# Shifting where the tensor engine's operands begin inside a 256-byte period of SBUF

## The chip, the cores and the metric

The kernel runs on one core of one Trainium2 chip. The metric is the device time of one execution in microseconds (us): the median over the runs shown, beside one profiled execution from which all rows below come.

## The reference, cut to what matters

Two transformer blocks in sequence, on one sequence of 512 tokens with model width 1024, in float32. The first block has four attention branches (stick-breaking, block-sparse, forgetting, top-k), gates on them, and a feed-forward net with a convolution of three taps. The second block is run for two layers: a feed-forward net, a mixer with four parts (latent attention, spatial gating, a gated recurrence, retention), a second feed-forward net and a gated side input.

```python
y = sigmoid(xn @ w_gate[i]) * (merge_heads(branches[i]) @ w_branch[i])     # first block, i = 0 to 3
hdn = xn @ w_up                                                            # 1024 -> 5632, then conv, gelu, @ w_down
h = h + 0.5 * swiglu(rmsnorm_2(h, ffn1_norm[l]), w_gate[l], w_up[l], w_down[l])   # twice a layer, 1024 -> 2816 -> 1024
z = rmsnorm_2(h, mix_norm[l]) @ w_in[l]
```

By far most of the arithmetic is the product of the 512 tokens with weight matrices.

## The kernel before, in words

**The weight stream.** All weights of the networks and projections are cut into 504 pieces of 128 partitions x 1024 floats (4096 bytes of a partition). SyncE (SP) loads a piece into one of two slots of `raw`, by two DMAs (`piece`, L494), as soon as the piece two before it has been split. GpSimd (POOL) splits it: L678 rounds `raw` into `wh` (type fp32r), L685 writes the rest `raw - wh` into `wl`, in four instructions of 256 columns. Both have two slots. TensorE (PE) then multiplies. The activations are split in the same way into a rounded part and a rest: `xh` and `xl` for the normed input, `op_hi` and `op_lo` for four more rows of operands, and areas of the large buffer `arena` (under its second name `arena_rounded`) for `yh`, `yl`, `mh`, `ml` and most of the hidden rows of the networks. Each product of a block of 128 weights' columns with 512 tokens is three matmuls of fp32r: `wh` with the rounded part, `wh` with the rest, `wl` with the rounded part. These are L728, L729 and L737 (`products`), L1269, L1270 and L1277 (the down projections), L775, L776 and L780 (`fm_steps`), L850, L851 and L858, L1180, L1181 and L1187. In L876, L877 and L885 the roles are exchanged: the stationary operand is a block of tokens and the moving one a block of 2 x 128 weights.

Every such matmul has a weight load of its own (LDWEIGHTS, 128 x 128), which runs while the matmul before it streams.

**Other work on TensorE.** Attention, the recurrence, transposes and sums of squares take their operands from `arena`, `const` and `ones` as plain float32.

**What sets the order.** The order on each engine is written out by hand; engines wait for each other by semaphores. The lists `BEHIND`, `AHEAD` and `LAST` say which piece's product stands behind which step of the attentions. Piece by piece, POOL's L678 waits for the DMAs of its piece and for PE's last use of `wh` two pieces ago (`rounded_read`), L685 for PE's last use of `wl` two pieces ago (`pieces_used`), PE for POOL.

**Where things lie.** The tensors are allocated one behind another in SBUF, each beginning at a multiple of 32 bytes. What follows calls the remainder of a beginning by 256 bytes its *residue*. Rows of 512 floats and blocks of 128 or 1024 floats are multiples of 256 bytes, so inside `wh`, `wl`, `xh`, `xl`, `op_hi`, `op_lo` and `raw` every operand has its tensor's residue. The kernel asserts these beginnings in three places:

```python
    assert arena_at % 256 == 0, arena_at % 256
    ...
    assert nc.sbuf_base % 256 == 0, nc.sbuf_base % 256
    xh, xl = sb("xh", [P, DC, S], F32R), sb("xl", [P, DC, S], F32R)
    ...
    sb("between", [P, 40])
    assert nc.sbuf_base % 256 == 0, nc.sbuf_base % 256
    wh, wl = sb("wh", [P, 2, PIECE], F32R), sb("wl", [P, 2, PIECE], F32R)
```

Before the change: `arena` 0, `xh`, `xl`, `op_hi`, `op_lo`, `raw`, `wh`, `wl` 0, `h` 160, `const` 32, `ones` and `nrm` 128. Inside `arena` not every area keeps residue 0: `total` (input of the sums of squares, L901) 0; `lprob` (transposed at L943) 0; `prob` (transposed at L984) 128, because `dsv` before it has 288 floats; `gnt` (moving operand of some of L1490) 64, because `dend` and `minus_ends` before it have 8 floats each; the stationary matrix of L1581, `R("centre")`, 184; `conv` 32 and the four rows of `padded` (514 floats each) 0, 8, 16 and 24, both used at L2002; `hS` and `hk` (L2038) 0.

Of the kernel before, what the change touches and what calls it, by code (L numbers as in the profile page):

```python
# [30 lines left out]
P = 128  # L31
# [208 lines left out]
def program(nc, x, out, k, scratch, book):  # L240
# [3 lines left out]
    def sb(name, shape, dt=F32):  # L244
        return ctx.enter_context(nc.sbuf_tensor(name, shape, dt))
# [21 lines left out]
    stat = sb("stat", [P, 2, 4])  # L267
    assert nc.sbuf_base % 256 == 0, nc.sbuf_base % 256

    xh, xl = sb("xh", [P, DC, S], F32R), sb("xl", [P, DC, S], F32R)  # L270
    op_hi, op_lo = sb("op_hi", [P, 4, S], F32R), sb("op_lo", [P, 4, S], F32R)

    raw = sb("raw", [P, 2, PIECE])
# [1 line left out]
    const = sb("const", [P, CONST_N])  # L275

    ident16, mask16 = sb("ident16", [P, P], BF16), sb("mask16", [P, P + 2], BF16)
    sb("between", [P, 40])
    assert nc.sbuf_base % 256 == 0, nc.sbuf_base % 256
    wh, wl = sb("wh", [P, 2, PIECE], F32R), sb("wl", [P, 2, PIECE], F32R)  # L280
    lcol = sb("lcol", [P, LAYERS * L_NROWS])
    ones = sb("ones", [P, 3, P])
# [2975 lines left out]
def build(nc, arrays, known=None):  # L3258

    k = {n: nc.dram_tensor(f"in_{n}", a.shape, mybir.dt.from_np(a.dtype), kind="ExternalInput").ap()  # L3260
         for n, a in arrays.items()}
    out = nc.dram_tensor("out_0", (1, S, D), F32, kind="ExternalOutput").ap()
    scratch = nc.dram_tensor("t5_by_distance", (8, 640), F32).ap()
    book = Book(known)
    program(nc, k["x"][0], out[0], k, scratch, book)
    return book
# [20 lines left out]
```

## Time and profile before

| what | value |
|---|---|
| median of 3 runs | 3042.71 us (3041.12 to 3046.15) |
| profiled execution, its own time | 3041.56 us |
| its span, first to last instruction | 3040.3 us |
| TensorE busy | 3003.6 us (99%), 14934 matmuls |
| LDWEIGHTS busy | 2432.5 us (80%) |
| VectorE busy | 1415.7 us (47%) |
| ScalarE busy | 724.5 us (24%) |
| GpSimd busy | 2176.3 us (72%) |
| moved by DMA | 272.90 MB, mean 90 GB/s |
| mean granted TensorE clock | 0.998 |

Matmuls overlap in the profile: the duration of one reaches from its start until its last result, and the next begins before that. So the rate is read from the distance between two starts, not from the duration. Busy time is the union of such spans.

### The profile page before, as it was taken

The page shows a single profiled execution, that of the slowest core. Times are in us where ns is not written, and L with a number is a line of the kernel's source. Part 1 is how long each engine was busy: PE and PEld are TensorE (multiplying, and loading weights), DVE is VectorE, ACT ScalarE, POOL GpSimd, SP SyncE. Part 2 cuts the span into 40 slices and gives each one's busy share as a digit, 9 for nine tenths or more (in the row PEclk, how much of TensorE's full clock was granted, in tenths as well). Part 3 has the DMA queues.
Part 4 walks back from the last instruction along what each step waited for, and adds up shares of the span by engine and source line. Part 5 has one row for each costly group of instructions (what it writes and reads, how often), then busy time and mean ns, then how long its engine had stood idle before and what let it go on. Part 6 is the DMA issues. An engine that isn't in the chain of part 4 may idle for free.

```text
span 3040.3 us, 39415 instructions
## 1 busy us (share of the span) xinstructions
PE 3003.6 (99%) x14934; PEld 2432.5 (80%) x14934; DVE 1415.7 (47%) x2157; ACT 724.5 (24%) x1434; POOL 2176.3 (72%) x2524
## 2 busy tenths in 40 slices
PE   9999999999999999999999999999999999999998
PEld 7776777888888888887788888888888877888886
DVE  5467556777156421476732212622213767422214
ACT  3433222222021100344411101311002444111003
POOL 6665668988788877754487777877777554877775
PEclk9999999999999999999999999999999999999999
DMA  5322223333333333322133333333323221333332
GB/s 162 79 67 63 77 80 91 97 97 97 99 100 104 97 97 97 92 55 62 56 99 97 97 103 97 94 98 97 98 96 94 63 55 54 100 97 98 104 97 83
DMA packets 469205, 272.90 MB, mean 90 GB/s; under 512 B 20798, under 2 KB 465136, under 8 KB 469016
## 3 DMA queue, kind: packets, MB, share of 16 engines
q1 hardware_dynamic: 466904, 267.22, 29.7%
q10 hardware_dynamic: 2112, 3.17, 0.3%
q8 instruction: 118, 1.93, 0.3%
q14 instruction: 71, 0.58, 0.1%
HBM read 268.21 MB, written 2.12 MB: 89 GB/s over the span
## 4 chain that ended last, share of the span: by engine, by line
PE 86%; DVE 3%; ACT 1%; issue 0%; DVEq 0%; ACTq 0%
PE bank L728 17%; PE bank L729 17%; PE bank L737 17%; PE bank L1269 7%; PE bank L1277 7%; PE bank L1270 7%; PE bank L850 2%; PE bank L858 2%; PE bank L851 1%; PE bank L775 1%; PE bank L776 1%; DVE arena L2343 1%; PE bank L780 1%; PE bank L1122 1%; PE bank L1442 1%; PE bank L885 1%
## 5 line engine op out<-in xcount | busy, mean ns | idle before, releaser
L685 POOL TENSOR_TENSOR wl<-raw,wh 128x256 fp32r<-128x256 f32 x2016 | 1617.0, 832 | 286.0 <-PE bank L737 182.2
L678 POOL TENSOR_SCALAR wh<-raw 128x1024 fp32r<-128x1024 f32 x504 | 562.8, 1117 | 555.4 <-PE bank L729 170.2
L728 PE MATMUL bank<-xh,wh 128*128 128x512 f32 x1552 | 610.7, 393 | 0.0
L729 PE MATMUL bank<-xl,wh 128*128 128x512 f32 x1552 | 604.3, 389 | 0.0
L2343 DVE TENSOR_TENSOR arena<-bank,nrm 128x512 f32<-128x512 f32 x236 | 152.4, 685 | 541.9 <-PE bank L737 541.7
L737 PE MATMUL bank<-xh,wl 128*128 128x512 f32 x1552 | 390.6, 391 | 0.0
L2343 DVE TENSOR_TENSOR arena<-arena 128x512 f32<-128x512 f32 (+1 forms) x373 | 339.1, 915 | 59.5 <-ACT arena L2059 11.7
L728 PEld LDWEIGHTS bank<-xh,wh 128*128 128x128 f32 x1552 | 291.7, 188 | 62.7 <-issue 2.1
L737 PEld LDWEIGHTS bank<-xh,wl 128*128 128x128 f32 x1552 | 289.9, 188 | 64.6 <-issue 4.6
L729 PEld LDWEIGHTS bank<-xl,wh 128*128 128x128 f32 x1552 | 291.5, 188 | 60.4 <-issue 1.2
L728 PE MATMUL bank<-arena_rounded,wh 128*128 128x512 f32 x824 | 321.7, 390 | 1.0 <-DVE arena L2343 1.0
L729 PE MATMUL bank<-arena_rounded,wh 128*128 128x512 f32 x824 | 320.6, 389 | 0.0
L2352 DVE SCALAR_TENSOR_TENSOR h<-bank,h 128x512 f32<-128x512 f32 x64 | 44.3, 692 | 481.0 <-PE bank L1277 445.9
L1269 PE MATMUL bank<-arena_rounded,wh 128*128 128x512 f32 x592 | 230.7, 390 | 0.0
L1270 PE MATMUL bank<-arena_rounded,wh 128*128 128x512 f32 x592 | 230.3, 389 | 0.0
L1991 ACT ACTIVATE arena<-arena 128x512 f32<-128x512 f32 x88 | 55.7, 633 | 682.6 <-DVE arena L2343 682.6
L737 PE MATMUL bank<-arena_rounded,wl 128*128 128x512 f32 x824 | 203.5, 389 | 0.0
L728 PEld LDWEIGHTS bank<-arena_rounded,wh 128*128 128x128 f32 x824 | 154.7, 188 | 34.0 <-DVE arena L2343 1.4
L729 PEld LDWEIGHTS bank<-arena_rounded,wh 128*128 128x128 f32 x824 | 154.7, 188 | 32.4 <-issue 0.5
L737 PEld LDWEIGHTS bank<-arena_rounded,wl 128*128 128x128 f32 x824 | 154.7, 188 | 32.1
L1277 PE MATMUL bank<-arena_rounded,wl 128*128 128x512 f32 x592 | 161.5, 389 | 0.0
L1277 PEld LDWEIGHTS bank<-arena_rounded,wl 128*128 128x128 f32 x592 | 111.1, 188 | 23.2
(370 smaller groups left out, 4098.6 us busy)
## 6 DMA issues: line engine op xcount, KB each, us to landing
raw<-in_ffn_w_gate SPq DMA_DIRECT2D x176, 256.0 KB, 3.1
raw<-in_ffn_w_up SPq DMA_DIRECT2D x176, 256.0 KB, 3.1
raw<-in_ffn_w_down SPq DMA_DIRECT2D x176, 256.0 KB, 2.9
raw<-in_w_in SPq DMA_DIRECT2D x158, 256.0 KB, 3.1
raw<-in_w_up SPq DMA_DIRECT2D x88, 256.0 KB, 3.2
raw<-in_w_gate SPq DMA_DIRECT2D x64, 256.0 KB, 3.1
raw<-in_w_out SPq DMA_DIRECT2D x48, 256.0 KB, 3.0
raw<-in_w_down SPq DMA_DIRECT2D x44, 256.0 KB, 2.9
```

The costliest lines, as they stand in the source:

```text
L678: pool.tensor_scalar(wh[:, s, :], raw[:, s, :], 1.0, 0.0, ALU.mult, ALU.add).then_inc(split, 1)
L685: ins = pool.tensor_tensor(wl[:, s, c], raw[:, s, c], wh[:, s, c].bitcast(F32), ALU.subtract)
L728: pe.matmul(psum, cols(wh, i), xhi, start=(i == 0), stop=False)
L729: ins = pe.matmul(psum, cols(wh, i), xlo, start=False, stop=False)
L737: ins = pe.matmul(psum, cols(wl, i), xhi, start=False, stop=(i == last))
L850: pe.matmul(o, cols(wh, i), xhi, start=(i == 0), stop=False)
L858: ins = pe.matmul(o, cols(wl, i), xhi, start=False, stop=(i == last))
L1269: pe.matmul(bank[2 * s + b][:, :], w, xhi, start=(kk == 0 and i == 0), stop=False)
L1270: ins = pe.matmul(bank[2 * s + b][:, :], w, xlo, start=False, stop=False)
L1277: ins = pe.matmul(bank[2 * s + b][:, :], cols(wl, i, b), hid[2 * kk + i][0], start=False, stop=end)
L1991: act.activation(t, t, other_table(ACT.Silu)).then_inc(*A.up("silu", tag, n))
L2343: v.tensor_tensor(out, a, b, op).then_inc(*V.up(*what))
```

## The change

Two unused tensors are put ahead of `xh` and of `op_hi`, and an unused one ahead of `wh` is made smaller. Nothing else is changed: every instruction, its shape and order, every DMA and every wait stays. The whole diff:

```diff
@@ -267,7 +267,9 @@
     stat = sb("stat", [P, 2, 4])
     assert nc.sbuf_base % 256 == 0, nc.sbuf_base % 256
 
+    sb("before_x", [P, 16])
     xh, xl = sb("xh", [P, DC, S], F32R), sb("xl", [P, DC, S], F32R)
+    sb("before_op", [P, 40])
     op_hi, op_lo = sb("op_hi", [P, 4, S], F32R), sb("op_lo", [P, 4, S], F32R)
 
     raw = sb("raw", [P, 2, PIECE])
@@ -275,8 +277,8 @@
     const = sb("const", [P, CONST_N])
 
     ident16, mask16 = sb("ident16", [P, P], BF16), sb("mask16", [P, P + 2], BF16)
-    sb("between", [P, 40])
-    assert nc.sbuf_base % 256 == 0, nc.sbuf_base % 256
+    sb("between", [P, 8])
+    assert nc.sbuf_base % 256 == 96, nc.sbuf_base % 256
     wh, wl = sb("wh", [P, 2, PIECE], F32R), sb("wl", [P, 2, PIECE], F32R)
     lcol = sb("lcol", [P, LAYERS * L_NROWS])
     ones = sb("ones", [P, 3, P])
```

The residues after it, worked out from the sizes:

| tensor | before | after |
|---|---|---|
| `arena`, `h` | 0, 160 | 0, 160 |
| `xh`, `xl` | 0 | 64 |
| `op_hi`, `op_lo` | 0 | 224 |
| `raw` (DMA target, POOL's input) | 0 | 224 |
| `const` | 32 | 0 |
| `wh`, `wl` | 0 | 96 |
| `ones`, `nrm` | 128 | 224 |

## Rows read from the trace of the kernel before

**Rows 1.** The page: span, and busy time of TensorE (share, instructions).
```profile
span 3040.3 us, 39415 instructions
...
PE 3003.6 (99%) x14934; PEld 2432.5 (80%) x14934; DVE 1415.7 (47%) x2157; ACT 724.5 (24%) x1434; POOL 2176.3 (72%) x2524
```

**Rows 2.** The page, the chain that ended last: shares of the span by line.
```profile
PE bank L728 17%; PE bank L729 17%; PE bank L737 17%; PE bank L1269 7%; PE bank L1277 7%; PE bank L1270 7%; PE bank L850 2%; PE bank L858 2%; PE bank L851 1%; PE bank L775 1%; PE bank L776 1%; DVE arena L2343 1%; PE bank L780 1%; PE bank L1122 1%; PE bank L1442 1%; PE bank L885 1%
```

**Rows 3.** The page, costliest groups: busy us, mean ns | idle before, releaser.
```profile
L728 PE MATMUL bank<-xh,wh 128*128 128x512 f32 x1552 | 610.7, 393 | 0.0
...
L728 PE MATMUL bank<-arena_rounded,wh 128*128 128x512 f32 x824 | 321.7, 390 | 1.0 <-DVE arena L2343 1.0
...
L1277 PE MATMUL bank<-arena_rounded,wl 128*128 128x512 f32 x592 | 161.5, 389 | 0.0
```

**Rows 4.** Windows of 60 us: us, busy (count) by engine, clock, DMA share, GB/s.
```profile
1000.00:1060.00 60.00, 60.00 (x266) 49.68 (x265) 21.22 (x27) 7.59 (x12) 46.56 (x56) 1.00 0.33 97
2200.00:2260.00 60.00, 60.00 (x267) 49.67 (x266) 9.99 (x11) 5.00 (x8) 45.15 (x56) 1.00 0.30 97
```

**Rows 5.** Timeline of a down projection: start, duration (us), engine, line, operation.
```profile
2225.73 0.39 PE L1269 MATMUL bank<-arena_rounded,wh 128*128 128x512 f32 x1
2225.74 0.19 PEld L1270 LDWEIGHTS bank<-arena_rounded,wh 128*128 128x128 f32 x1
...
2227.09 0.39 PE L1269 MATMUL bank<-arena_rounded,wh 128*128 128x512 f32 x1
```

**Rows 6.** Plain float32 matmuls of 512 columns, by line: duration min/median/max in ns.
```profile
L901 PEld LDWEIGHTS bank<-arena,ones x20: 187/188/192, 519.8 to 2978.4; 128*128 128x128 f32 x20
L901 PE MATMUL bank<-arena,ones x20: 590/592/594, 520.0 to 2978.8; 128*128 128x512 f32 x20
...
L1490 PEld LDWEIGHTS bank<-arena,const x16: 186/191/193, 1367.8 to 2557.2; 128*128 128x128 f32 x16
L1490 PE MATMUL bank<-arena,const x16: 590/594/697, 1367.8 to 2557.6; 128*128 128x512 f32 x16
...
L1581 PE MATMUL bank<-arena x8: 592/619/697, 1454.4 to 2550.7; 128*128 128x512 f32 x8
```

**Rows 7.** Transposes of 128 x 128, by line: duration min/median/max in ns.
```profile
L943 PE MATMUL bank<-const,arena x80: 270/272/329, 1402.8 to 2561.6; 128*128 128x128 f32 x80
...
L984 PE MATMUL bank<-const,arena x160: 271/273/331, 56.5 to 434.2; 128*128 128x128 f32 x160
```

**Rows 8.** ScalarE activations of 512 columns with scale and bias columns, by line.
```profile
L2002 ACT ACTIVATE arena<-arena,pcol,convw x44: 799/814/822, 527.5 to 751.1; 128x512 f32<-128x512 f32 x44
...
L2038 ACT ACTIVATE arena<-arena,lbs x8: 800/808/817, 1251.3 to 2346.5; 128x512 f32<-128x512 f32 x8
```

**Rows 9.** Timeline of GpSimd over two pieces; in brackets its idle time before.
```profile
1016.22 1.10 POOL L678 TENSOR_SCALAR wh<-raw 128x1024 fp32r<-128x1024 f32 x1 [0.35 <-PE bank L729]
1018.02 2.82 POOL L685 TENSOR_TENSOR wl<-raw,wh 128x256 fp32r<-128x256 f32 x4 [0.70 <-PE bank L737]
1021.66 1.05 POOL L678 TENSOR_SCALAR wh<-raw 128x1024 fp32r<-128x1024 f32 x1 [0.82 <-PE bank L729]
```

**Rows 10.** Timeline of SyncE: issues of a piece's two DMAs.
```profile
1015.89 0.92 SPq L494 DMA_DIRECT2D raw<-in_ffn_w_up  x2
1020.87 0.92 SPq L494 DMA_DIRECT2D raw<-in_ffn_w_gate  x2
```

**Rows 11.** GpSimd's waits: us in total, times, longest us.
```profile
POOL wl L685 <- PE bank L737: 182.2, 251, 2.1
...
POOL wh L678 <- DMA raw<-in_w_in: 14.0, 5, 7.4
```

**Rows 12.** DMA issues of one weight matrix: count, KB each, median us to landing.
```profile
raw<-in_ffn_w_up SPq DMA_DIRECT2D x176, 256.0 KB, 3.1
```

**Rows 13.** The window of the first 76 us, columns as in Rows 4.
```profile
0.00:76.00 76.00, 69.31 (x365) 56.80 (x366) 43.26 (x66) 29.94 (x63) 47.20 (x60) 1.00 0.54 162
```

**Rows 14.** TensorE's longest wait.
```profile
PE bank L1442 <- DVE arena L2343: 7.4, 6, 2.1
```

## The prediction

> **What bounds the kernel now.** I read first the page's head: TensorE is busy 3003.6 of 3040.3 us [rows 1]. Busy alone says little, since matmuls overlap. So next the chain that ended last: it runs almost wholly through TensorE's lines, half of it through L728, L729 and L737 [rows 2]; the same lines head the costliest groups, with practically no idle time before them [rows 3]. Then two windows of 60 us, one of a gate/up stage and one of a down projection: 266 and 267 matmuls at clock 1.00 [rows 4], so one starts about every 0.225 us. The timeline gives it exactly: from 2225.73 to 2227.09 lie six distances, 1.36 / 6 = 0.2267 us, and the next weight load starts 0.01 us behind each matmul [rows 5]. At the full clock of 2.4 GHz 512 columns last 213.3 ns. So each matmul costs its columns and a **surplus of 13.3 ns**. The trace has 11,472 matmuls of this kind (fp32r, 512 columns; the first and the last large groups are in [rows 3]) and 888 of 256 columns. 11,472 x 0.2267 = 2601 us, 86% of the span. TensorE's longest wait sums to 7.4 us [rows 14]. Only what alters that distance, or a new wait of TensorE, can move the time: 0.5 ns on each of these matmuls is already 5.7 us, about the 0.2% that a measurement of this kernel can tell from no change.
>
> **The change, part by part.** It adds and removes no instruction, DMA or wait; it moves beginnings. So each part is the price of reading or writing at another residue.
>
> *1. TensorE reads `xh`, `xl` at 64, `op_hi`, `op_lo` at 224 and the weights at 96.* In the trace every fp32r operand has residue 0, so the price isn't shown. The nearest rows are plain float32 matmuls of the same 512 columns at other residues: L901 (stationary 128, moving 0), L1490 (stationary 32, moving 64 or 0) and L1581 (stationary 184, moving 0) have minima of 590, 590 and 592 ns, and their loads medians of 188 and 191 [rows 6]. The longer ones, up to 697, are the first of a pair behind a matmul of another kind. Transposes whose stationary operand is at 0 (L943) or 128 (L984) have medians of 272 and 273 ns [rows 7]. No residue shows in these. They are another data type, so they bound the price at nothing but don't prove it. From above: 13.3 ns, the surplus once more, 11,472 x 13.3 = +153 us. From below: the surplus vanishes, -153 us. I take 0, since rows 6 and 7 are the same engine reading the same memory, and nearer to this case than either bound.
>
> *2. The DMAs write `raw` at 224.* A piece's DMAs are issued at 1015.89 [rows 10]; with a landing of 3.1 us behind the second issue [rows 12] they are there by about 1019.9 (0.92 + 3.1 later). POOL takes up that piece at 1021.66, released by TensorE [rows 9]. So 1.8 us are free, over half of the landing. The DMA engines are a third busy [rows 4]. If all of a landing's time grew by half, 1.5 us, it would still be hidden here. The cover is thin in two places: POOL waited for a DMA of `w_in` five times, 14.0 us together [rows 11], and the first 76 us have a DMA share of 0.54 [rows 13]. Were each of those five waits half a landing longer: 5 x 1.5 = 7.5 us of POOL, at most as much of the end. From below 0; nothing there gets faster by it. I take +0.3 us for the first pieces.
> By the Trainium skill ("DMA: Bandwidth & Descriptors", How a descriptor splits into AXI transactions) a descriptor that doesn't start at a multiple of 256 bytes pays for the bytes below its start; by its table's counting I estimate 23 beats instead of 16 for 512 bytes at 224. That rule speaks against the change; no row here shows a packet at another residue. If it holds for the written side, the sum gets the few us of the bound above and no more.
>
> *3. POOL reads `raw` at 224 and writes and reads `wh`, `wl` at 96.* Per piece it works 1.10 + 2.82 us of 5.44 (1021.66 - 1016.22) and waits for TensorE in between [rows 9]; over the stretch 46.56 of 60 us [rows 4], and its waits for L737 alone sum to 182.2 us [rows 11]. No row shows POOL at another residue. Bounds: nothing, and 60 / 46.56 = 1.29 times slower, below which TensorE doesn't wait in steady state. I take 0. Beyond 1.29, what's late next is `wl` for L737.
>
> *4. ScalarE and VectorE write `xh`, `xl`, `op_hi`, `op_lo` and use `nrm`, `const` at new residues.* Here the trace has a direct comparison: L2002 reads rows at 0, 8, 16 and 24 and writes at 32, L2038 reads and writes at 0; 814 and 808 ns [rows 8]. At most 6 ns, on engines busy 24% and 47% [rows 1], on no long wait of TensorE. I take 0; both signs are below 1 us.
>
> Sum: 0 + 0.3 + 0 + 0, so the profiled execution's 3041.6 becomes 3041.9. It stands 1.1 us below the median of the runs, 3042.7; I forecast 3043.
>
> **The rivals.**
> *A, slower: fp32r reads do care.* A moving row of 2048 bytes at residue 64 touches nine stretches of 256 bytes instead of eight, a block of 512 bytes of weights at 96 touches three instead of two. The plain float32 matmuls are longer (590 against 389 ns), so they may take their data more slowly and have room that fp32r has not; rows 6 don't exclude it. Price: the only step that the groups show between matmuls of this form is 393 against 389 ns [rows 3]; 4 ns x 11,472 = 46 us, 3089 us, and with the upper bound of part 1 3196. It decides from 0.5 ns on. For it: all fp32r operands lie at 0, where nothing can be seen, and they are 86% of the span. Against it: rows 6 and 7. Chance 0.26.
> *B, faster: the surplus comes from equal residues.* Today the matmul's and the next load's operands both begin at 0 and start within 0.01 us of each other [rows 5]. Afterwards they differ by 32 (`xh`), 128 (`op_hi`) and 96 (`arena`). If the 13.3 ns came from this meeting, they'd be gone: 3043 - 153 = 2890. Against it: two streams that collide once would be out of step by one access and stay so; 32 cycles are too many. Chance of all of it 0.05, of a part (1 to 3 ns, 11 to 34 us, 3009 to 3032) 0.11.
> The Trainium skill ("TensorE: Matmul & The Clock Gate", Wait - 56ns, not 53.3ns?) gives back-to-back starts at the full clock as columns plus about 2.5 ns, 11 ns below what the timeline shows. By that figure alone the room of B would be 126 us; the row's own columns give 153.
> *C, slower: loads turn late.* Landing must grow by more than the 1.8 us of part 2 to reach the steady state; then each piece would wait. With 1 us too much on 504 pieces it would be 3547, which nothing hints at. Short of that, the thin places give up to 7.5 us, 3050. Chance of more than 0.2% 0.04. POOL beyond 1.29 times (part 3) gives the same picture, chance 0.02.
> *D, the change isn't one.* Allocation might be rearranged so that nothing moves; the asserts make that improbable, and it gives 3043 as well, within my forecast.
>
> **How the numbers follow.** Within 0.2% (3036.6 to 3048.8): 0.52, D among it. Slower: A 0.26 + C and POOL 0.06 = 0.32. Faster: B 0.16. The likeliest is no measurable change: 3043 us, its own range 3037 to 3049. To hold 8 in 10 the range must take in the middle of A (3089) and a part above it, and the smaller part of B: 3025 to 3105. Inside are 0.52 + 0.06 (C, POOL) + 0.05 (half of B's part) + 0.17 (A up to 5 ns) = 0.80; left out are all of the surplus gone (0.05), the rest of B's part, and A above 5 ns.
>
> **What would show it.** Right: six distances between matmul starts of a down projection are again 1.36 us; the 60 us windows hold 266 and 267 matmuls; L728's mean stays at 389 to 393 ns; L2002 stays at 814. Right also, but for part 2: packets take longer, landing above 3.1 us, and TensorE's waits don't grow. Wrong: fewer than 265 matmuls in such a window (A), more than 268 (B); a difference between `xh` and `arena_rounded` rows would say which residue pays. Waits of TensorE for POOL, or of POOL for DMA above 14 us, would show C.

## The result: 2.3% slower, and the profile after

The changed kernel takes 3112.15 us (median of 4 runs, 3110.8 to 3113.83) against 3042.78 us before (4 runs, 3041.12 to 3046.15). The ratio is 1.0227, with an interval of 1.0209 to 1.0245. That lies above the range that was given (3025 to 3105). It is rival A by its sign and by its place on TensorE, but 69 us instead of 46.

The page of the kernel after, first its head, then lines of its costliest groups (busy us, mean ns | idle before, releaser). The lines of code stand two further down than before: L730, L731 and L739 are L728, L729 and L737.

```profile
span 3110.3 us, 39415 instructions
PE 3074.2 (99%) x14934; PEld 2434.5 (78%) x14934; DVE 1413.3 (45%) x2157; ACT 724.8 (23%) x1434; POOL 2167.1 (70%) x2524
...
L730 PE MATMUL bank<-xh,wh 128*128 128x512 f32 x1552 | 619.7, 399 | 0.0
L730 PE MATMUL bank<-arena_rounded,wh 128*128 128x512 f32 x824 | 327.7, 398 | 0.8 <-DVE arena L2345 0.8
L1279 PE MATMUL bank<-arena_rounded,wl 128*128 128x512 f32 x592 | 166.0, 397 | 0.0
```

The count of instructions is the same as in [rows 1], but TensorE is busy 70.6 us longer and the span is 70.0 us longer. All other engines work as long as before, within 10 us. The mean of every group of over 150 us rose by 6 to 8 ns (three of them against [rows 3]), and the idle time ahead of them stayed nil. The two windows of 60 us that answer to [rows 4]:

```profile
1000.00:1060.00 60.00, 60.00 (x259) 48.31 (x258) 31.46 (x38) 8.17 (x13) 47.14 (x55) 1.00 0.33 97
2200.00:2260.00 60.00, 60.00 (x259) 48.33 (x257) 12.56 (x16) 5.06 (x8) 42.91 (x54) 1.00 0.29 91
```

The clock is 1.00 as before, and 259 matmuls fit where 266 and 267 did. The prediction had named this as the mark of rival A ("fewer than 265"). The timeline (start, duration in us) shows the distance:

```profile
1001.86 0.40 PE L730 MATMUL bank<-xh,wh 128*128 128x512 f32 x1
1002.09 0.40 PE L731 MATMUL bank<-xl,wh 128*128 128x512 f32 x1
...
1002.79 0.40 PE L730 MATMUL bank<-xh,wh 128*128 128x512 f32 x1
```

From the first to the last of these starts lie four distances, 0.93 us, so 232.5 ns each; before, [rows 5] gave 226.7 for the `arena` rows, and the table below has 227.35 for these. And the plain float32 lines on which the forecast of "nothing" rested (duration min/median/max in ns):

```profile
L903 PE MATMUL bank<-arena,ones x20: 590/592/593, 528.6 to 3047.8; 128*128 128x512 f32 x20
...
L1492 PE MATMUL bank<-arena,const x16: 592/592/697, 1397.8 to 2613.8; 128*128 128x512 f32 x16
...
L986 PE MATMUL bank<-const,arena x160: 270/272/330, 58.3 to 440.4; 128*128 128x128 f32 x160
```

`ones` moved from 128 to 224 and `const` from 32 to 0, and the minima and medians of these lines haven't moved by more than 2 ns from [rows 6, 7]. So the engine's plain float32 matmuls take as long as before, and its fp32r ones don't.

**The sum.** The mean distance from the start of an fp32r matmul to the start of the next matmul of any kind (distances under 250 ns alone), times the count, gives the whole loss. "Difference" is the residue of the moving operand minus that of the stationary one, modulo 256:

| matmuls | count | difference after | ns before | ns after | us |
|---|---|---|---|---|---|
| `arena` by `wh`/`wl`, 512 columns | 4560 | 160 | 226.77 | 234.24 | +34.1 |
| `xh`/`xl`, 512 | 5904 | 224 | 227.35 | 233.23 | +34.7 |
| `op_hi`/`op_lo`, 512 | 1008 | 128 | 227.54 | 232.26 | +4.8 |
| twice 128 of `wh`/`wl` by `xh`/`xl` | 768 | 32 | 125.80 | 123.64 | -1.7 |

Together +71.9 us against the span's +70.0. Nothing else is needed to account for the result. (The means of the last line include distances to matmuls of other kinds; between two of these matmuls alone, without the doubled distances where a record is missing, it is 119.7 before and 117.4 after. The saving is the same.) This last line is a surprise: the matmuls of L878, L879 and L887, where the weights are the moving operand (two rows of 128) and `xh` or `xl` the stationary one, got faster. Their durations show it too: 274/280/286 ns for L879 against 277/283/287 for the same line before.

### The profile page after: what moved, and what is told of

Its sections match the earlier page's. It is cut to its first block, busy times and chain, and to the rows that moved or that the text cites. A ratio compares the mean times of both kernels' runs of the same rounds, so it can differ in the third digit from the quotient of the medians.

```text
span 3110.3 us, 39415 instructions
## 1 busy us (share of the span) xinstructions
PE 3074.2 (99%) x14934; PEld 2434.5 (78%) x14934; DVE 1413.3 (45%) x2157; ACT 724.8 (23%) x1434; POOL 2167.1 (70%) x2524
## 4 chain that ended last, share of the span: by engine, by line
PE 93%; DVE 3%; ACT 2%; issue 1%; POOL 1%; DMA 0%; SPq 0%; DVEq 0%; POOLq 0%; ACTq 0%
PE bank L730 18%; PE bank L739 18%; PE bank L731 18%; PE bank L1279 7%; PE bank L1272 7%; PE bank L1271 7%; PE bank L852 2%; PE bank L860 2%; PE bank L853 1%; DVE arena L2345 1%; PE bank L777 1%; PE bank L778 1%; PE bank L1124 1%; PE bank L782 1%; PE bank L922 1%; PE bank L887 1%
## 5 line engine op out<-in xcount | busy, mean ns | idle before, releaser
L687 POOL TENSOR_TENSOR wl<-raw,wh 128x256 fp32r<-128x256 f32 x2016 | 1612.2, 831 | 312.6 <-PE bank L739 211.5
L730 PE MATMUL bank<-xh,wh 128*128 128x512 f32 x1552 | 619.7, 399 | 0.0
L731 PE MATMUL bank<-xl,wh 128*128 128x512 f32 x1552 | 613.6, 395 | 0.0
L739 PE MATMUL bank<-xh,wl 128*128 128x512 f32 x1552 | 400.2, 397 | 0.0
L739 PEld LDWEIGHTS bank<-xh,wl 128*128 128x128 f32 x1552 | 290.2, 188 | 73.8 <-issue 4.6
L730 PEld LDWEIGHTS bank<-xh,wh 128*128 128x128 f32 x1552 | 291.9, 188 | 71.3 <-issue 1.4
L731 PEld LDWEIGHTS bank<-xl,wh 128*128 128x128 f32 x1552 | 291.8, 188 | 69.2 <-issue 1.2
L730 PE MATMUL bank<-arena_rounded,wh 128*128 128x512 f32 x824 | 327.7, 398 | 0.8 <-DVE arena L2345 0.8
L731 PE MATMUL bank<-arena_rounded,wh 128*128 128x512 f32 x824 | 326.6, 396 | 0.0
L1271 PE MATMUL bank<-arena_rounded,wh 128*128 128x512 f32 x592 | 234.9, 397 | 0.0
L1272 PE MATMUL bank<-arena_rounded,wh 128*128 128x512 f32 x592 | 234.6, 396 | 0.0
L739 PE MATMUL bank<-arena_rounded,wl 128*128 128x512 f32 x824 | 209.8, 396 | 0.0
L730 PEld LDWEIGHTS bank<-arena_rounded,wh 128*128 128x128 f32 x824 | 155.2, 188 | 39.4 <-DVE arena L2345 1.2
L731 PEld LDWEIGHTS bank<-arena_rounded,wh 128*128 128x128 f32 x824 | 155.2, 188 | 38.1 <-issue 0.5
L739 PEld LDWEIGHTS bank<-arena_rounded,wl 128*128 128x128 f32 x824 | 155.2, 188 | 37.8
L1279 PE MATMUL bank<-arena_rounded,wl 128*128 128x512 f32 x592 | 166.0, 397 | 0.0
```

The source lines that it names most:

```text
L687: ins = pool.tensor_tensor(wl[:, s, c], raw[:, s, c], wh[:, s, c].bitcast(F32), ALU.subtract)
L730: pe.matmul(psum, cols(wh, i), xhi, start=(i == 0), stop=False)
L731: ins = pe.matmul(psum, cols(wh, i), xlo, start=False, stop=False)
L739: ins = pe.matmul(psum, cols(wl, i), xhi, start=False, stop=(i == last))
L1271: pe.matmul(bank[2 * s + b][:, :], w, xhi, start=(kk == 0 and i == 0), stop=False)
L1272: ins = pe.matmul(bank[2 * s + b][:, :], w, xlo, start=False, stop=False)
```

## The experiments

The ratios compare an experiment with runs of the kernel before on the same chip. `sN` and `mN` are stationary and moving operands; the probes hold no part of the network, only matmuls behind one load of `x`.

**e1_pairs.** All 64 pairs of eight stationary and eight moving residues, fp32r, 64 matmuls each. Letters a to h are residues 0, 32, ... 224.

```diff
+        for s in range(8):
+            for m in range(8):
+                ins = run(s, m, RUN)
```

> Matmuls alone: eight stationary tensors and eight moving ones, each at residues 0, 32, ... 224, 64 matmuls of fp32r with 512 columns for each of the 64 pairs, nothing else running; the rest of the reference's computation is left out. Pairing theory (the distance between starts depends on the two residues together): about 227 ns wherever they are equal, 229 to 240 ns elsewhere, the eight equal pairs alike. Crossing theory (a row or block that doesn't begin at 0 touches one more stretch of 256 bytes): 227 ns only at (0, 0), all of the row or column of residue 0 in between, and equal pairs at other residues as slow as unequal ones. Late loads: 227 ns everywhere, since no DMA and no GpSimd runs beside it.

Measured (costliest groups of the probe; busy us of 64 matmuls, mean ns):

```profile
L62 PE MATMUL bank<-mb,sa 128*128 128x512 f32 x64 | 15.1, 395 | 0.0
L62 PE MATMUL bank<-mf,sa 128*128 128x512 f32 x64 | 15.2, 396 | 0.0
L62 PE MATMUL bank<-ma,sd 128*128 128x512 f32 x64 | 15.2, 396 | 0.0
L62 PE MATMUL bank<-mc,sa 128*128 128x512 f32 x64 | 14.8, 391 | 0.0
L62 PE MATMUL bank<-mf,sd 128*128 128x512 f32 x64 | 14.8, 391 | 0.0
L62 PE MATMUL bank<-mb,sb 128*128 128x512 f32 x64 | 14.7, 389 | 0.0
L62 PE MATMUL bank<-md,sd 128*128 128x512 f32 x64 | 14.7, 389 | 0.0
L62 PE MATMUL bank<-mh,sh 128*128 128x512 f32 x64 | 14.7, 389 | 0.0
```

Busy time less the last duration, over 63, is the distance: (14.7 - 0.39) / 63 = 227 ns for `mb,sb`, `md,sd`, `mh,sh`; (15.2 - 0.40) / 63 = 235 for `mf,sa` and for `ma,sd`. The 64 cells depend on the **difference** alone (one cell is 1 ns off):

| difference | 0 | 32 | 64 | 96 | 128 | 160 | 192 | 224 |
|---|---|---|---|---|---|---|---|---|
| ns per matmul | 226.7 | 233.3 | 228.9 | 233.3 | 233.3 | 234.3 | 233.3 | 233.3 |

All eight equal pairs give the floor. Rival A's mechanism, that a row beginning off a multiple of 256 touches one stretch more, is refuted: `md,sd` touches it and stays at the floor.

**e2_weights_96 and e3_all_96.** The weights alone at 96; then everything at 96, that is equal again but off the multiple.

```diff
-    sb("between", [P, 40])
-    assert nc.sbuf_base % 256 == 0, nc.sbuf_base % 256
+    sb("between", [P, 40 + 24])
+    assert nc.sbuf_base % 256 == 96, nc.sbuf_base % 256
```
```diff
+    sb("before_all", [P, 24])
     arena_at = (nc.sbuf_base + 31) // 32 * 32
-    assert arena_at % 256 == 0, arena_at % 256
+    assert arena_at % 256 == 96, arena_at % 256
```

> Only the weights' parts move, to 96; all activations stay at 0. Pairing theory: every pair is unequal, as in the changed kernel, so the distance is 232 to 235 ns and the time 3100 to 3125 us. Crossing theory: only the weight loads cross (three stretches for two); if they are what pays, 3112 as in the changed kernel, if the moving rows pay, 3043. Late loads: 3043 to 3050, since raw stays at 0.

> Everything from the large buffer on is moved by the same 96 bytes: weights' parts, networks' operands, small operands, raw and the large buffer all at 96. Pairing theory: all pairs are equal again, 226.7 ns, 3043 us (3037 to 3049). Crossing theory: every row and block crosses, at least as slow as the changed kernel, 3112 us or more. Late loads: near 3112, since raw is off the multiple too.

Measured: e2 3120.38 us, ratio 1.0261 (1.0244 to 1.0278); e3 3045.93 us, ratio 1.0013 (1.0004 to 1.0023). The window from 1000 us, of e2 and then of e3:

```profile
1000.00:1060.00 60.00, 60.00 (x258) 48.24 (x257) 31.29 (x37) 7.52 (x12) 46.79 (x54) 1.00 0.33 97
```
```profile
1000.00:1060.00 60.00, 60.00 (x267) 49.67 (x265) 21.19 (x27) 7.66 (x13) 46.84 (x57) 1.00 0.33 98
```

The weights alone cost more than the change did: every difference at 512 columns is then 160 (234.1 to 234.3 ns for all three kinds of operand), while the change put `xh` at 224 and `op_hi` at 128, both a little cheaper. With all at 96 the distances are those of before (226.77, 227.33, 227.53). This pair shows it in the kernel itself: the distances grow only where the residues of weights and activations differ, not with either residue by itself. (e3's 4 us are not in these distances. Part of them goes with the granted clock: it is 0.996 to 0.998 in the ten runs of e3 and 0.997 to 0.999 in the runs of before. At 0.997 the means are 3045.9 against 3042.9 us, so 3 us, 0.1%, stay unexplained.)

**e4_x_64.** `xh` and `xl` at 64, the rest at 0; the small tensors change places to make room.

```diff
+    eps = sb("eps", [P, 1])
+    mask16 = sb("mask16", [P, P + 2], BF16)
+    assert (nc.sbuf_base + 31) // 32 * 32 % 256 == 64
     xh, xl = sb("xh", [P, DC, S], F32R), sb("xl", [P, DC, S], F32R)
```

> Only xh and xl move, to 64; weights, small operands, raw and the large buffer stay at 0 (some small tensors are laid elsewhere for room). Pairing theory: matmuls with xh and xl (about 5800 of 11472) take 229 to 236 ns, those with the large buffer stay at 226.7; the time rises by 5800 x 2 to 9 ns = 12 to 52 us, 3055 to 3095. Crossing theory: the same sign if moving rows pay, 3043 if only weight loads pay. Late loads: 3043.

Measured: 3051.15 us, ratio 1.0034 (1.0021 to 1.0047), +9.4 us. That is under the range expected. By distances: 227.35 to 229.14 ns on 5904 matmuls, +10.6 us; `op` +1.1; and twice 128 columns from 125.80 to 121.92 ns on 768, -3.0. Sum +8.7. e1's 228.9 for this difference holds in the kernel. The expectation had taken 2 to 9 ns where this difference costs 1.8, and had not counted the saving on the short ones.

**e5_fine.** The moving row begins at 64 places 4 bytes apart, stationary at 0. Names `mXY`: X stands for 32-byte steps, Y for 4-byte steps (`mab` begins at 4).

```diff
+        for m in range(64):
+            ins = run(m, RUN)
```

> Matmuls alone, 64 of fp32r with 512 columns for each of 64 moving operands that begin 0, 4, 8, ... 252 bytes behind a multiple of 256, with the weights' block at 0; the rest of the computation is left out. What the pairs at steps of 32 bytes gave: 226.7 ns at a difference of 0, 228.9 at 64, 234.3 at 160, 233.3 at the others. Theory of whole lines (the collision is between accesses of 16 or 32 bytes): the 4-byte steps inside a line change little, below 1 ns, and no difference is faster than 226.7. Theory that equal residues are only the best of a coarse grid: some difference between gives less than 226.7, down to the 213.3 ns of the columns, which would be worth up to 11472 x 13.3 = 153 us. Crossing theory is out by the pairs; it would have 226.7 at 0 alone and one higher value elsewhere.

```profile
L64 PE MATMUL bank<-meb,s 128*128 128x512 f32 x64 | 15.5, 404 | 0.0
L64 PE MATMUL bank<-mab,s 128*128 128x512 f32 x64 | 15.3, 399 | 0.0
L64 PE MATMUL bank<-mca,s 128*128 128x512 f32 x64 | 14.8, 391 | 0.0
L64 PE MATMUL bank<-mah,s 128*128 128x512 f32 x64 | 14.7, 388 | 0.0
L64 PE MATMUL bank<-mhe,s 128*128 128x512 f32 x64 | 14.7, 388 | 0.0
```

The cost can change within 4 bytes: 226.7 ns at 0, 236.7 at 4 (`mab`), 233.3 at 8, 226.7 again at 28 (`mah`) and 240 at 132 (`meb`). So it isn't a matter of whole lines of 16 or 32 bytes, as one expectation had it. And nothing of the 64 is below 226.7, so the other expectation fails too: at 512 columns no place tried gives back any of the surplus of 13.3 ns. Seven places other than 0 reach the floor here: 28, 60, 108, 156, 236, 240 and 252. e13 comes back to them.

**e6_widths.** Other widths of the moving operand, stationary at 0.

```diff
+        for width in (512, 384, 256, "pair", 192, 128):
+            for m in range(8):
+                ins = run(m, width, RUN)
```

> Matmuls alone at 512, 384, 256, 2 x 128, 192 and 128 columns, moving operand at 0, 32, ... 224, weights' block at 0; the rest of the computation is left out. If the surplus over the columns is a price of each weight load (it reads 128 columns beside the stream, whatever the stream's length), it stays 13 ns at equal residues at every width and 16 to 21 ns at the others, until the load itself becomes the bound. If it is a price of the stream (a share of all its accesses collide), it shrinks with the columns: 7 ns at 256. The changed kernel's rows, 117 to 118 ns for 2 x 128 where 120 were before, speak for an order among the differences that is another one at 256 columns.

```profile
L68 PE MATMUL bank<-ma,s 128*128 128x256 f32 x128 | 15.7, 283 | 0.0
L68 PE MATMUL bank<-mg,s 128*128 128x256 f32 x128 | 14.8, 276 | 0.0
L68 PE MATMUL bank<-ma,s 128*128 128x384 f32 x64 | 11.3, 334 | 0.0
L68 PE MATMUL bank<-mf,s 128*128 128x384 f32 x64 | 11.5, 340 | 0.0
L68 PE MATMUL bank<-ma,s 128*128 128x192 f32 x64 | 7.3, 274 | 0.0
L68 PE MATMUL bank<-mf,s 128*128 128x192 f32 x64 | 7.3, 273 | 0.0
```

| columns | 0 | 32 | 64 | 96 | 128 | 160 | 192 | 224 |
|---|---|---|---|---|---|---|---|---|
| 384 | 173.3 | 173.3 | 173.3 | 176.7 | 176.0 | 176.7 | 174.7 | 173.6 |
| 256, or twice 128 | 119.8 | 117.8 | 117.8 | 119.9 | 118.7 | 117.3 | 113.3 | 118.3 |
| 192 and 128 | 111.7 | 111.7 | 111.7 | 111.7 | 111.7 | 111.7 | 111.7 | 111.7 |

At difference 0 the surplus is 13.3 ns whatever the columns (384: 160.0 + 13.3; 256: 106.7 + 13.1; the columns at 2.4 GHz). That agrees with a fixed price for each weight load, one of the two expectations, but only there: at 256 columns a difference of 192 leaves 6.6 of the 13.1 ns. Which difference is the best depends on the width: 0 is the best at 512 and nearly the worst at 256. It also accounts for the twice-128 matmuls of the kernel, whose difference goes the other way round (weights minus `x`): it is 32 after the change, where the probe saves 2.0 ns and the kernel 2.2; 96 in e2, where the probe has +0.1 and the kernel 0.0; 192 in e4, where the probe saves 6.5 and the kernel 3.9. At 192 and below nothing depends on the residue, and 64 columns more or less change nothing either. So the columns don't set the distance there; that the weight loads do is likely, and not shown.

**e7_raw_224.** `raw` alone at 224, which is part 2 of the prediction by itself.

```diff
+    assert (nc.sbuf_base + 31) // 32 * 32 % 256 == 224
+    raw = sb("raw", [P, 2, PIECE])
+    sb("gap0", [P, 8])
```

> Only raw moves, to 224; all of TensorE's fp32r operands stay at 0 (some small tensors are laid elsewhere for room). Pairing theory: 226.7 ns and 3042 us within 0.3%. Late loads (the DMA's writes and GpSimd's reads at 224 cost something that reaches the end): up to 3050 us, with DMA packets or landings longer than before and TensorE's waits grown.

Measured: 3043.16 us, ratio 1.0 (0.9991 to 1.0009). Its DMA issues (KB each, median us to landing) and its window from 1000 us:

```profile
raw<-in_ffn_w_up SPq DMA_DIRECT2D x176, 256.0 KB, 3.3
```
```profile
1000.00:1060.00 60.00, 60.00 (x266) 49.68 (x265) 21.23 (x28) 8.19 (x13) 46.67 (x57) 1.00 0.35 103
```

Landing takes 3.3 us instead of 3.1 [rows 12], as in the kernel after, and the same number of matmuls fits as in [rows 4]. So the DMAs' writes and POOL's reads of `raw` at 224 have no part in the 69 us.

**e8_overlap.** Is it the matmul's own two operands that must agree, or the moving operand and the *next* weights, which load beside it? The residues alternate between 0 and k, so that one or the other agrees.

```diff
+                i, r = n // 2 % BLOCKS, k * (n % 2)
+                ins = pe.matmul(bank[0][:, :], still[r][:, i * P:i * P + P], move[r][:, n % 2 * S:n % 2 * S + S],
...
+                ins = pe.matmul(bank[0][:, :], still[k - r][:, i * P:i * P + P], move[r][:, n % 2 * S:n % 2 * S + S],
```

> Matmuls alone, residues alternating between 0 and k from one matmul to the next, for k = 32 to 224; the rest of the computation is left out. First 448 matmuls whose own moving and stationary operands have equal residues, so that the load that runs beside each stream has the other one; then 448 whose moving operand equals the residue of the next matmul's stationary operand, and differs from its own. If the collision is between a stream and the load that overlaps it: first group 229 to 234 ns in the mean (about 232.5), second 226.7. If what counts is a matmul's own two operands: the other way round.

Measured: own operands equal 228.4 to 234.1 ns (mean 232.2); next weights equal 230.0 to 231.5. Neither form returns to 226.7, so neither theory holds as it was stated. That matmuls whose own operands agree are slow when the weights next to be loaded don't speaks for the overlap with the load; but then the second form should have been at the floor. In both forms the residues also jump from one matmul to the next, which they do in no run of e1, and no run here has that jump alone. This stays open.

**e9_types.** The same eight moving residues in bf16 and in plain float32, stationary at 0.

```diff
+        for m in range(8):
+            ins = run(short_s, short[m], RUN)
+        for m in range(8):
+            ins = run(plain_s, plain[m], RUN // 2)
```

> Matmuls alone with 512 columns: 64 of bfloat16 and 32 of plain float32 for each moving residue 0 to 224, stationary at 0; the rest of the computation is left out. If the collision needs four bytes per column at one column a cycle for both readers, plain float32 and bfloat16 show no residue: bfloat16 near 216 ns at all eight, float32 within 2 ns of 427 per half at all eight (as the rows of L901 and L1490 were alike). If it is any two reads beside each other, they show steps of several ns as fp32r does.

```profile
L72 PE MATMUL bank<-fb,fs 128*128 128x512 f32 x64 | 27.6, 592 | 0.0
L72 PE MATMUL bank<-fa,fs 128*128 128x512 f32 x64 | 27.6, 592 | 0.0
L72 PE MATMUL bank<-ff,fs 128*128 128x512 f32 x64 | 27.6, 592 | 0.0
L72 PE MATMUL bank<-bb,bs 128*128 128x512 bf16 x63 | 13.9, 379 | 0.1
L72 PE MATMUL bank<-bf,bs 128*128 128x512 bf16 x63 | 13.9, 379 | 0.1
```

No difference between the eight residues in either type: 429.2 ns for each half of a plain float32 matmul, 216 ns for bf16. Of the three types only fp32r depends on them at these steps of 32 bytes; finer steps were tried for fp32r alone. This is where the prediction's proxy broke.

**e10_fine_2x128.** The form of two rows of 128 at 64 begins.

```diff
+                ins = pe.matmul(bank[0][:, 0:256], still[:, i * P:i * P + P], move[m][:, :, 0:P], start=(n == 0),
+                                stop=(n == count - 1))
```

> Matmuls alone, fp32r with 2 x 128 columns, 64 for each of 64 moving operands at 0, 4, ... 252 bytes behind a multiple of 256, stationary at 0; the rest of the computation is left out. At steps of 32 bytes it was 119.9 at 0 and 113.3 at 192. A stream and load that collide by their difference: again no smooth curve, between 113 and 122 ns, 113 to 115 somewhere near 196 (worth knowing, since 512 columns were at their floor of 226.7 for a difference of 60, and the two forms have the roles exchanged, so -60 = 196).

```profile
L65 PE MATMUL bank<-mag,s 128*128 128x256 f32 x64 | 8.2, 289 | 0.0
L65 PE MATMUL bank<-mae,s 128*128 128x256 f32 x64 | 7.6, 279 | 0.0
L65 PE MATMUL bank<-mga,s 128*128 128x256 f32 x64 | 7.4, 276 | 0.0
```

From 113.3 ns at 192 (`mga`) to 126.2 at 24 (`mag`), with 116.7 at 16 (`mae`) and 120.0 at 0. A trough around 192 was expected; 196 is at 122.2, so there is none, just single good places. The best place, difference 192, is the one that e4 had given these matmuls (`x` at 64, weights at 0): there it brought 3.0 us, and cost 10.6 at 512 columns. So for this kernel the two widths want different places, and the wider one decides.

**e11_x_240 and e12_x_4.** Two places of e5 were tried in the kernel: 240, at the floor of 226.7 ns for 512 columns, and 4, at 236.7. Would the fine table carry over? `xh` and `xl` become slices of one tensor, 16 bytes behind 224, or 4 bytes behind 0.

```diff
+    both = sb("both", [P, 4 + 2 * DC * S], F32R)
+    xh = both[:, 4:4 + DC * S].rearrange("p (c t) -> p c t", c=DC)
```
```diff
+    both = sb("both", [P, 1 + 2 * DC * S], F32R)
+    xh = both[:, 1:1 + DC * S].rearrange("p (c t) -> p c t", c=DC)
```

> Only xh and xl move, to 240, that is to a difference of 240 from the weights; the rest stays at 0. The pairs measured alone gave 226.7 ns for 512 columns at 240, as at 0, and for 2 x 128 with roles exchanged (difference 16) 116.7 where 0 gave 120.0. If differences are all that counts: 5904 x 0 and 768 x -3.3 ns = -2.5 us, 3039 us, ratio 0.9992, at most as fast as that; the rows of xh and wh keep 226.7. If only equal residues are good in the full kernel: 5904 x 2 to 7 ns = 12 to 41 us slower.

> Only xh and xl move, by 4 bytes, to 4. The pairs measured alone gave 236.7 ns at 4 for 512 columns and 120.0 for 2 x 128 at 252. If differences are all that counts, at a grain of 4 bytes: 5904 x 10.0 = +59 us, 3101 us (3090 to 3110). If the kernel cared for lines of 16 or 32 bytes only: 3042.

Measured: e11 3092.87 us, ratio 1.0166 (1.0151 to 1.0181), a miss by over 50 us; e12 3093.17 us, ratio 1.0168 (1.0151 to 1.0185), within the range expected, 8 us below its middle: `xh` and `xl` rows stand at 236.63 ns, as in e5, which is 9.3 ns more than their 227.35 and not 10.0. Windows from 1000 us, of e11 and then of e12:

```profile
1000.00:1060.00 60.00, 60.00 (x256) 48.27 (x255) 29.62 (x36) 7.52 (x12) 45.89 (x53) 1.00 0.32 94
```
```profile
1000.00:1060.00 60.00, 60.00 (x256) 47.80 (x255) 29.48 (x37) 7.52 (x12) 45.72 (x53) 1.00 0.33 96
```

In e11 matmuls with `xh` started 235.93 ns apart, not 226.7. The place that was free in the probe isn't free in the kernel. What differs is the sequence: the probe read one and the same row again and again, the kernel takes turns between `xh`, `xl` and chunks, behind matmuls of another difference.

**e13_leads.** The same run of 64 matmuls, moving rows taking turns, behind 21 or 22 matmuls of difference 0 (L77), 96 (L82) or 160 (L87). Letters a to l are differences 0, 28, 60, 64, 96, 108, 156, 160, 192, 236, 240, 252.

```diff
+        for m in range(12):
+            lead(4, 21)
+            for n in range(RUN):
+                s, c, flags = blocks(n)
+                ins = pe.matmul(bank[0][:, :], still[:, s], move[m][:, c], **flags)
```

> Matmuls alone, fp32r with 512 columns, 64 for each of the differences 0, 28, 60, 64, 96, 108, 156, 160, 192, 236, 240 and 252, each three times: behind 21 matmuls at a difference of 0, behind 21 at 96, behind 22 at 160; the rest of the computation is left out. If a difference has one value whatever comes before: 226.7 at 0, 28, 60, 108, 156, 236, 240 and 252, 228.9 at 64, 233 to 234 at 96, 160 and 192, three times alike. If the matmuls before choose among several steady patterns: 0 stays at 226.7 (it did all through the kernel, in which everything comes before it), and among the differences off the steps of 32, above all 240, some show two values, 226.7 and about 234 to 236.

```profile
L77 PE MATMUL bank<-mb,s 128*128 128x512 f32 x64 | 14.9, 391 | 0.0
L77 PE MATMUL bank<-mf,s 128*128 128x512 f32 x64 | 14.9, 391 | 0.0
L77 PE MATMUL bank<-mk,s 128*128 128x512 f32 x64 | 15.1, 396 | 0.0
L87 PE MATMUL bank<-md,s 128*128 128x512 f32 x64 | 15.1, 397 | 0.0
L77 PE MATMUL bank<-md,s 128*128 128x512 f32 x64 | 14.8, 392 | 0.0
L82 PE MATMUL bank<-ma,s 128*128 128x512 f32 x64 | 14.7, 390 | 0.0
L82 PE MATMUL bank<-mk,s 128*128 128x512 f32 x64 | 14.7, 388 | 0.0
L87 PE MATMUL bank<-mk,s 128*128 128x512 f32 x64 | 14.7, 388 | 0.0
```

Difference 240 (`mk`) takes 233.3 ns behind 0, but 226.7 behind 96 and behind 160. Difference 64 (`md`) takes 228.9, 228.9 and 233.3. The same instructions thus run at two steady rates, and what went before chooses. Difference 0 was at 226.7 behind all three.

The larger part of e5's table fails for another reason. Of its seven floor places other than 0, six are above the floor here behind all three leads alike, against what either expectation said:

| difference | 28 | 60 | 108 | 156 | 236 | 240 | 252 |
|---|---|---|---|---|---|---|---|
| e5, one row again and again | 226.7 | 226.7 | 226.7 | 226.7 | 226.7 | 226.7 | 226.7 |
| e13, two rows in turns | 230.0 | 228.3 | 230.0 | 230.0 | 228.9 | 233.3 or 226.7 | 230.0 |

The leads don't choose there, so what is left between the two probes is that the moving rows take turns (and that e5 had other matmuls ahead of each run). No run has that alone. Together the two effects show why a table from a probe doesn't carry over for differences other than 0. e11's 236 for difference 240 stays unmatched (at that difference no lead here gave more than 233.3).

**Measured against the sum of distances.** For each version of the kernel the counts of fp32r matmuls times its own mean distances less those of before, and the measured median less that of before:

| kernel | differences (`arena`, `x`, `op`) | sum of distances, us | measured, us |
|---|---|---|---|
| after | 160, 224, 128 | +71.9 | +69.4 |
| e2 | 160, 160, 160 | +81.4 | +78.7 |
| e12 | 0, 4, 0 | +54.9 | +51.1 |
| e11 | 0, 240, 0 | +50.2 | +50.9 |
| e4 | 0, 64, 0 | +9.1 | +9.4 |
| e3 | 0, 0, 0 | +0.5 | +4.2 |
| e7 | 0, 0, 0 | +0.1 | +0.8 |

The distances account for each version within 4 us. No version was faster than the kernel before.

## Why the prediction was wrong, point by point

**What bounds it: right.** TensorE's distance between starts was named as the only thing that could move the time, apart from a new wait, and it is what moved.

**Part 1, "I take 0": this is the step that failed.** It went by rows 6 and 7 as "the same engine reading the same memory, and nearer to this case than either bound". They are plain float32 rows, and e9 shows that plain float32 and bf16 don't depend on the residue, at the same eight residues where fp32r goes from 226.7 to 234.3 ns. The rows carried no information on the question; being close in operation wasn't being close in what limits it. The text said that they "don't prove it", and still gave them twice the chance of A. That every fp32r operand of the trace began at 0 was itself the warning: a value without any variation in it has nothing to say on what variation costs. In place of 0 the term measures +71.9 us, 6.4 ns on a 512-column matmul on average ((34.1 + 34.7 + 4.8) / 11,472).

**Rival A: right in sign and size class, wrong in mechanism.** It forecast +46 us from 4 ns a matmul. Its reason, one more stretch of 256 bytes per row, is refuted by e3, where all rows touch one more, and by the diagonal of e1. Its guess that the plain float32 matmuls may take their data more slowly and "have room that fp32r has not" fits e9, which shows that they don't care, but not why. The range ended at 3105 since A was cut off at 5 ns, and that 4 ns came from two duration means [rows 3] of which neither was a rate. (Nor are they the only step of the groups: L850, of the same form, has a mean of 417 ns before.)

**Rival B: the opposite is true at 512 columns.** Equal residues are not the source of the surplus but its floor, among all 64 begins tried. The reason that was held against B isn't borne out either: the two streams were to fall out of step after one collision and stay so, but at a difference of 32 the distance stayed at 233.3 ns, 6.6 above the floor, over all 64 matmuls of a run (e1). At 256 columns B is right in part: a difference of 192 takes the surplus from 13.1 to 6.6 ns (e6), and the change itself made 768 matmuls 2.2 ns shorter. (The 126 us that B had room for by the other surplus go by 11 ns; unrounded it is 10.8 ns and 124 us.)

The Trainium skill ("SBUF — State Buffer", A bandwidth-pool intuition that's wrong (but worth ruling out)) lists a second independent read port of PE for LDWEIGHTS beside the moving operand's. For bf16 e9 agrees (216 ns at each of the eight residues). By two independent reads alone fp32r shouldn't depend on how the moving operand stands to the weights, and it does (226.7 to 240.0 ns, e5): there the measurement decides, and e8 leaves open where the two meet. The Trainium skill gives a back-to-back distance of columns plus about 2.5 ns ("TensorE: Matmul & The Clock Gate", Wait — 56ns, not 53.3ns?), which the prediction weighed: bf16 keeps to it (213.3 + 2.5 = 215.8 against 216), fp32r doesn't (226.7).

**Part 2 (+0.3 us): right as far as it can be told.** Landing rose from 3.1 to 3.3 us, hidden. e7 has it alone at a ratio of 1.0 (0.9991 to 1.0009), so 0.3 us is too little to be seen. The 23 beats instead of 16 that the prediction had estimated for a packet don't show: the mean packet of 512 bytes took 28.3 ns before, 28.4 in e7 and in the kernel after. **Rival C** didn't happen, though its sign was set too near: POOL's waits for `w_in` (us in total, times, longest) are 15.9 us against 14.0 [rows 11], above the 14 that were to show C, and 15.4 in e7. They didn't reach TensorE, whose largest wait didn't grow (part 4).

```profile
POOL wh L680 <- DMA raw<-in_w_in: 15.9, 5, 7.8
```

**Part 3 (0): right.** POOL was busy 2167.1 us against 2176.3 [rows 1], and waits longer for TensorE than before (L739, 211.5 us against 182.2 of [rows 11]), as an engine does whose consumer has slowed.

**Part 4 (0): right.** ScalarE and VectorE were busy 724.8 and 1413.3 us against 724.5 and 1415.7. L2004 has a median of 810 ns against 814 [rows 8]. TensorE's largest wait sums to 7.0 us against 7.4 [rows 14].

**Rival D** is out: the distances did change.

## What to carry to other kernels

Where fp32r operands meet in a matmul of 512 columns, let them begin at the same residue modulo 256, each chunk of them too, and hold it with an assertion: in this kernel a difference cost 1.8 to 9 ns of 227 on each such matmul, up to 2.6% of the whole. At other widths try the places out: at 256 columns equal residues were not the best. When a change moves something that has only one value in the trace, rows of another data type don't bound its price; give the unshown price its weight, or measure it. Read the rate from distances of starts (or the count in a fixed window), and take no table from a probe that repeats one row for a kernel in which rows take turns.

## What the runs showed of the hardware that had not been expected

- The time of an fp32r matmul depends on the residues of its operands relative to each other, in steps as fine as 4 bytes: 226.7 to 240.0 ns at 512 columns (e5), 113.3 to 126.2 ns at twice 128 (e10). The residue in itself doesn't change the distance (e1's diagonal, e3), and bf16 and plain float32 don't show it at steps of 32 bytes (e9).
- Its best place turns with the width: difference 0 is the best at 512, difference 192 at 256 columns (113.3 against 119.8), and at 192 and 128 columns there is none, all at 111.7 (e6).
- At one and the same difference there are two or more steady rates, and the matmuls before choose between them (e13: 226.7 or 233.3 at 240). Others are slower when two rows take turns than with one row repeated (28, 108, 156 and 252: 230.0 in e13, 226.7 in e5). What the two streams collide in, and why e11 settled at 236, remain open: e8 separated the matmul's own weights from the next ones and satisfied neither theory.
- The surplus of 13.3 ns over the columns at fp32r was the same at 512 and 384 columns, and no placing at 512 columns reduced it; at 256 columns it was 13.1 and went down to 6.6 at a difference of 192. Where it comes from wasn't found.
